# The first two chunks of a Strassen feed-forward: order of adds, tiles, splits and copies

## What is computed

```
def swiglu(h, w_gate, w_up, w_down):
    return (jax.nn.silu(h @ w_gate) * (h @ w_up)) @ w_down

def reference(x, ...):
    for i in range(DEPTH):                       # DEPTH = 2
        hn = rms_norm(x, norm_mix_g[i])
        x = x + gmlp_mixer(...)  or  x + chunk_attention(...)
        hn = rms_norm(x, norm_ffn_g[i])
        x = x + swiglu(hn, ffn_w_gate[i], ffn_w_up[i], ffn_w_down[i])
    return rms_norm(x, final_g)
```

## Time and profile before

| | us |
|---|---|
| median of 3 runs | 2608.01 (2607.97 to 2608.17) |
| the profiled execution, its own time | 2607.87 |
| its span in the trace | 2606.1 |
| TensorE busy | 2459.5 (94%) |
| VectorE / ScalarE / GpSimd busy | 1684.9 / 1002.8 / 1295.1 |
| mean granted TensorE clock | 0.986 |

### The profile page before, as it was taken

One profiled execution on the slowest core, in us unless ns is written; L12 is line 12 of the kernel. 1 busy time (PEld: TensorE's weight loads), 2 busy tenths in 40 slices (PEclk: granted clock), 3 DMA queues, 4 the chain that ended last, 5 costly groups with the idle time before them and its releaser, 6 DMA issues. The chain is left out here.

```text
span 2606.1 us, 36363 instructions
## 1 busy us (share of the span) xinstructions
PE 2459.5 (94%) x11464; PEld 2024.2 (78%) x11464; DVE 1684.9 (65%) x2669; ACT 1002.8 (38%) x1815; POOL 1295.1 (50%) x908
## 2 busy tenths in 40 slices
PE   8998999999899999998889999999888999999997
PEld 6887888877688888876767777777766888888876
DVE  5246666667576777666756666676675667677756
ACT  4112111224344333331465555566642334433323
POOL 4242223222788787877212012221125877888776
PEclk9998999999999999999999999999999999999998
DMA  4223122111111211111110011111011111111111
GB/s 161 92 98 98 61 76 74 58 35 37 44 58 48 62 51 57 56 55 42 59 35 25 26 42 42 42 38 39 13 41 29 57 56 56 48 60 53 57 57 65
DMA packets 70522, 143.74 MB, mean 55 GB/s; under 512 B 7312, under 2 KB 17696, under 8 KB 69936
## 3 DMA queue, kind: packets, MB, share of 16 engines
q1 hardware_dynamic: 52912, 119.72, 14.3%
q10 hardware_dynamic: 17536, 23.07, 2.6%
HBM read 130.13 MB, written 12.63 MB: 55 GB/s over the span
## 5 line engine op out<-in xcount | busy, mean ns | idle before, releaser
L703 POOL TENSOR_TENSOR a_lo<-raw_block,a_hi 128x512 fp32r<-128x512 f32 x364 | 510.3, 1402 | 152.1 <-ACT a_hi L1554 128.0
L665 POOL TENSOR_SCALAR w_hi<-raw 128x1024 fp32r<-128x1024 f32 x80 | 91.1, 1139 | 847.0 <-PE bank L914 601.0
L1554 ACT ACTIVATE a_hi<-raw_block 128x512 fp32r<-128x512 f32 x312 | 195.9, 629 | 342.5 <-PE bank L914 143.7
L912 PE MATMUL bank<-T_hi,a_hi 128*128 128x512 f32 x672 | 264.0, 393 | 7.8 <-issue 7.1
L914 PE MATMUL bank<-T_hi,a_lo 128*128 128x512 f32 x672 | 263.1, 391 | 0.0
L913 PE MATMUL bank<-T_lo,a_hi 128*128 128x512 f32 x672 | 262.7, 391 | 0.0
L912 PE MATMUL bank<-B_hi,a_hi 128*128 128x512 f32 x576 | 225.2, 391 | 2.6 <-DVE h_full L2004 1.8
L914 PE MATMUL bank<-B_hi,a_lo 128*128 128x512 f32 x576 | 224.2, 389 | 0.0
L913 PE MATMUL bank<-B_lo,a_hi 128*128 128x512 f32 x576 | 224.2, 389 | 0.0
L667 POOL TENSOR_TENSOR w_lo<-raw,w_hi 128x1024 fp32r<-128x1024 f32 x80 | 198.4, 2480 | 6.7
L2004 DVE TENSOR_TENSOR h_full<-bank,h_full 128x512 f32<-128x512 f32 x54 | 37.3, 691 | 212.2 <-PE bank L914 211.8
(11 more groups left out here) (276 smaller groups left out, 6658.5 us busy)
## 6 DMA issues: line engine op xcount, KB each, us to landing
raw_block<-f_blocks_in SPq DMA_DIRECT2D x176, 256.0 KB, 2.6
raw<-w_units_in SPq DMA_DIRECT2D x80, 512.0 KB, 3.5
raw_block<-f_down_in SPq DMA_DIRECT2D x72, 256.0 KB, 3.0
v_raw<-v_scratch ACTq DMA_DIRECT2D x16, 512.0 KB, 3.9
bias<-rel_scratch ACTq DMA_DIRECT2D x8, 640.0 KB, 3.5
x<-x_t_in SPq DMA_DIRECT2D x16, 256.0 KB, 5.7
v_scratch<-atmp ACTq DMA_DIRECT2D x16, 256.0 KB, 2.6
v_scratch<-full ACTq DMA_DIRECT2D x16, 256.0 KB, 2.5
```

The lines of the kernel that those rows point to most:

```text
L665: pool.tensor_scalar(w_hi[slot][:, :], raw[r][:, :], 1.0, 1.0, ALU.mult, ALU.mult).then_inc(w_split, 1)
L703: pool.tensor_tensor(out, full, r32(hi), ALU.subtract).then_inc(made, 1)
L912: pe.matmul(out, lh, rh, start=start, stop=False, skip_group_check=read_between)
L1554: act.activation(a_hi[pos][:, :], src[:, :], ACT.Copy).then_inc(w.left_hi, 1)
```

## The change

- **Chunk 0, half 0 of the down product:** VectorE does the residual adds earlier among its preparations for half 1: two by two before, now single adds between `scaled`, `difference` and `right_lo`. The same instructions, another order.
- **Chunk 0, half 1:** TensorE takes B22 of feature tile 1 (banks 1, 3) in the k loop and tile 0 (banks 0, 2) behind it, bank by bank. All that follows takes tile 1 first: the additions, silu, the product, the high and low parts, and the down product. VectorE makes the sums T2, T3, T4 for all four k ahead of it, where two of four stood behind it. T3's low parts 1 to 3 now stand behind the first `cadd` of chunk 1.
- **Chunk 1's gate group** becomes a middle group: GpSimd leaves seven high parts to ScalarE's `left_high`, which gets them at the end of chunk 0. GpSimd and the last load start from product 10 (banks 1 and 3 done), not 12; ScalarE's high parts in slots 4 to 6 still wait for 12. SyncE loads the blocks for the up group in the order of a middle group, and TensorE waits by its numbers.
- **Chunk 1, ScalarE:** the high parts A11, A12 of the up group go behind the copy of bank 0 after S2, and the one of S2 behind the copy of bank 1 after S3, where each stood ahead of it.
- The counts of the semaphores `made` and `left_hi` are renumbered for every later chunk; nothing else of those is touched.

```diff
-MID_MADE = 20 + GROUP
+MID_MADE = 20 + MID
...
+AT_G0_SECOND = AT_G1 - 1
...
-sp.wait_ge(s.prod, 12)
+sp.wait_ge(s.prod, 10)
 block(1, 3, 3)
...
-gate_up(1, 1, lambda op: MADE_SECOND + MADE[op], first_order)
+gate_up(1, 1, lambda op: middle(1, AT_G0_SECOND, MID, MID_MADE + MIDDLE[op]), order)
...
-        pool.wait_ge(s.left_hi, middle(it, at, 7, slot + 1))
+        pool.wait_ge(s.left_hi, middle(it, at, 7, 7 + slot + 1))
...
-        pool.wait_ge(s.prod, N_PROD.first)
+        pool.wait_ge(s.prod, 10)
...
-        group(3, lambda op: MADE_SECOND + MADE[op], lambda op: None)
+        middle_group(it, AT_G0_SECOND)
...
         for up in range(2):
+            tile(bank[2 * up + 1], 5 + 2 * up, "B22", k, False, k == 3, s.prod if k == 3 else None)
+    for up in range(2):
+        for k in range(4):
             tile(bank[2 * up], 4 + 2 * up, "B22", k, False, k == 3, s.prod if k == 3 else None)
-    for k in range(4):
-        for up in range(2):
-            tile(bank[2 * up + 1], 5 + 2 * up, "B22", k, False, k == 3, s.prod if k == 3 else None)
-    down(0, "first", 1, 8, ((0, 3), (1, 4)))
+    down(0, "first", 1, 8, ((1, 3), (0, 4)))
...
-    for k in range(2):
+    for k in range(4):
         right_hi("T2", k, full_lo["T2"], 20 + 3 * k + 1)
         right_hi("T4", k, full_lo["T4"], 20 + 3 * k + 3)
     act.wait_ge(w.cadd, 1)
+    silu(held[:, 1, :], hidden_part(h_full, 1, 1))
+    hi(0, 3, 1, 1)
+    act.wait_ge(w.prod, 10)
+    for pos in range(2):
+        left_high(1, AT_G0_SECOND, pos)
+    act.wait_ge(w.cadd, 3)
     silu(held[:, 0, :], hidden_part(h_full, 0, 1))
-    hi(0, 3, 0, 1)
-    act.wait_ge(w.cadd, 3)
-    silu(held[:, 1, :], hidden_part(h_full, 1, 1))
-    hi(0, 4, 1, 1)
-    for k in range(2, 4):
-        right_hi("T2", k, full_lo["T2"], 20 + 3 * k + 1)
-        right_hi("T4", k, full_lo["T4"], 20 + 3 * k + 3)
+    hi(0, 4, 0, 1)
+    for pos in range(2, 4):
+        left_high(1, AT_G0_SECOND, pos)
+    act.wait_ge(w.prod, 12)
+    for pos in range(4, 7):
+        left_high(1, AT_G0_SECOND, pos)
     for k in range(4):
         right_hi("T3", k, full_lo["T3"], 32)
...
-        if kind == "second":
-            product(0, {slot: op for op, slot in SLOT.items()}[pos])
-            left_high(it, AT_G1, pos)
-        else:
-            product(0, ORDER[pos])
-            left_high(it, AT_D, pos)
+        product(0, ORDER[pos])
+        left_high(it, AT_G1 if kind == "second" else AT_D, pos)
...
     snap(bank[0], gated[0])
-    behind_gate(0)
     if kind != "second":
+        behind_gate(0)
         right_high(it - 1, "T1")
         right_high(it - 1, "T3")
-    behind_gate(1)
+        behind_gate(1)
     product(0, "S2")
     snap(bank[0], gated[1])
+    if kind == "second":
+        behind_gate(0)
+        behind_gate(1)
     act.wait_ge(w.cadd, N_CADD.at(it, 1))
     silu(gated[0][:, :], gated[0])
     if kind != "second":
         right_high(it - 1, "T2")
         right_high(it - 1, "T4")
-    behind_gate(2)
+        behind_gate(2)
     product(0, "S3")
     snap(bank[1], gated[2])
+    if kind == "second":
+        behind_gate(2)
     behind_gate(3)
     behind_gate(4)
...
-    for k in range(5):
-        if k < 4:
-            scaled(k, k, full_lo["T3"][:, k, :])
-            scaled(k, 4 + k, b22_full[:, k, :])
-        if k:
-            right_lo("T1", k - 1, full_lo["T2"], 8 + 2 * k)
-        if k < 4:
-            difference(full_lo["T2"], full_lo["T3"], full_lo["T2"], k, 8 + 3 * k + 1)
-        if k:
-            right_lo("B22", k - 1, b22_full, 8 + 2 * k)
-        if k < 4:
-            add(0, "first", 0, 0, 2 * k)
-            add(0, "first", 0, 0, 2 * k + 1)
-    t2_t3_t4(0)
-    t2_t3_t4(1)
+    def t3(k):
+        scaled(k, k, full_lo["T3"][:, k, :])
+
+    def b22(k):
+        scaled(k, 4 + k, b22_full[:, k, :])
+
+    def t1(k):
+        difference(full_lo["T2"], full_lo["T3"], full_lo["T2"], k, 8 + 3 * k + 1)
+
+    def t1_lo(k):
+        right_lo("T1", k, full_lo["T2"], 8 + 2 * (k + 1))
+
+    def b22_lo(k):
+        right_lo("B22", k, b22_full, 8 + 2 * (k + 1))
+
+
+    t3(0)
+    b22(0)
+    t1(0)
+    add(0, "first", 0, 0, 0)
+    add(0, "first", 0, 0, 1)
+    t1_lo(0)
+    add(0, "first", 0, 0, 2)
+    b22_lo(0)
+    add(0, "first", 0, 0, 3)
+    t3(1)
+    b22(1)
+    add(0, "first", 0, 0, 4)
+    t1(1)
+    add(0, "first", 0, 0, 5)
+    t3(2)
+    t1_lo(1)
+    add(0, "first", 0, 0, 6)
+    b22_lo(1)
+    add(0, "first", 0, 0, 7)
+    b22(2)
+    t1(2)
+    t3(3)
+    t1_lo(2)
+    b22_lo(2)
+    b22(3)
+    t1(3)
+    t1_lo(3)
+    b22_lo(3)
+    for k in range(4):
+        t2_t3_t4(k)
     t2_t4_lo(0)
     dve.wait_ge(w.prod, 9)
-    cadd(held[:, 0, :], bank[0])
+    cadd(held[:, 1, :], bank[1])
     dve.wait_ge(w.prod, 10)
-    cadd(held[:, 2, :], bank[2])
+    cadd(held[:, 3, :], bank[3])
     t2_t4_lo(1)
     dve.wait_ge(w.cadd, 2)
     dve.wait_ge(w.act, 3)
-    times(held[:, 2, :], 0, 1)
+    times(held[:, 3, :], 1, 1)
+    t2_t4_lo(2)
     dve.wait_ge(w.prod, 11)
-    cadd(held[:, 1, :], bank[1])
-    lo(0, 3, 0, 1)
+    cadd(held[:, 0, :], bank[0])
+    lo(0, 3, 1, 1)
     dve.wait_ge(w.prod, 12)
-    cadd(held[:, 3, :], bank[3])
+    cadd(held[:, 2, :], bank[2])
     dve.wait_ge(w.cadd, 4)
     dve.wait_ge(w.act, 4)
-    times(held[:, 3, :], 1, 1)
-    t2_t3_t4(2)
-    lo(0, 4, 1, 1)
-    add(0, "first", 1, 8, 0)
-    add(0, "first", 1, 8, 1)
-    t2_t3_t4(3)
-    add(0, "first", 1, 8, 2)
-    add(0, "first", 1, 8, 3)
-    t2_t4_lo(2)
-    add(0, "first", 1, 8, 4)
-    add(0, "first", 1, 8, 5)
-    t2_t4_lo(3)
-    add(0, "first", 1, 8, 6)
-    add(0, "first", 1, 8, 7)
+    times(held[:, 2, :], 0, 1)
+    right_lo("T2", 3, full_lo["T2"], 16 + 2 * 3 + 2)
+    lo(0, 4, 0, 1)
     for k in range(4):
+        add(0, "first", 1, 8, k)
+    right_lo("T4", 3, full_lo["T4"], 16 + 2 * 3 + 2)
+    for k in range(4, KT):
+        add(0, "first", 1, 8, k)
+    right_lo("T3", 0, full_lo["T3"], 24 + 1)
+    dve.wait_ge(w.prod, N_PROD.at(1, PROD["A12"]))
+    dve.wait_ge(w.snap, N_SNAP.at(1, 1))
+    cadd(gated[0][:, :], bank[1])
+    for k in range(1, 4):
         right_lo("T3", k, full_lo["T3"], 24 + k + 1)
...
-    product(0, "A12")
-    snap(1)
-    cadd(gated[0][:, :], bank[1])
     if kind != "second":
+        product(0, "A12")
+        snap(1)
+        cadd(gated[0][:, :], bank[1])
```

More of the change, by code:

```diff
@@ L132 @@
 N_PROD, N_SNAP, N_CADD = Count(12, 14), Count(4, 6), Count(4, 6)
-MADE_SECOND, MADE_LAST = 20, middle(LATE, AT_D_LATE, MID, MID_MADE + MID)
+MADE_FIRST, MADE_LAST = 20, middle(LATE, AT_D_LATE, MID, MID_MADE + MID)
 def ge(eng, sem, value):
@@ L1151, in first_chunk @@
                     spread(norm, 1)
-                    pe.wait_ge(s.made, MADE_SECOND)
+                    pe.wait_ge(s.made, MADE_FIRST)
                     down(0, "first", 0, 0, ((0, 1), (1, 2)))
@@ L1175, in made @@
                         elif kind == "second" and g == 0:
-                            pe.wait_ge(s.made, MADE_SECOND + MADE[op])
+                            pe.wait_ge(s.made, middle(it, AT_G0_SECOND, MID, MID_MADE + MIDDLE[op]))
                         else:
@@ L1212, in one @@
                             swapped = kind == "late" and g == 1
-                            by_gpsimd = kind == "second" and g == 0
                             for op in ("S4", "A22") if swapped else ("A22", "S4"):
                                 made(g, "lo " + op)
-                                slot = SLOT[op] if by_gpsimd else ORDER.index(op)
+                                slot = ORDER.index(op)
                                 if op == "A22":
```

## The result

| | us |
|---|---|
| changed kernel, median of 4 runs | 2587.68 (2584.94 to 2588.96) |
| kernel before, beside it | 2608.09 (2607.97 to 2610.88) |
| ratio | 0.9913, 95% interval 0.9898 to 0.9927 |
| profiled execution of the changed kernel, its time | 2588.96 |
| its span | 2586.8 (before 2606.1) |

The account below looks back on a forecast made before the run. TensorE's waits and slow clock around the first chunk's down product and second gate lose 16.5 us per feed-forward. Gate 6.3 us earlier (3.0 from adds) plus 4.6 gives 10.8, twice 21.6: 2607.87 becomes 2586.5, range 2576 to 2594.

Parts of the forecast that it names:

- Adds: Chunk 0, half 0 of the down product: TensorE's waits for residual adds go, 3.0 us won for each feed-forward.
- Tile 1 first: Chunk 0, half 1: hidden low parts ready at 654.3 and 659.3; TensorE idles 2.8 us first, then waits again.
- Low clock: Second half of the down product: 0.5 us added for slow clock after the first pause, between 0 and 2.
- GpSimd's early start: GpSimd's first sum at 649.1, amid VectorE's chain; SBUF-only VectorE instructions there cost 0.60 alone, up to 1.67 us beside it.
- B: Rival: VectorE and GpSimd hardly meet in half 1; gate at 663.1, 15.8 us for each feed-forward, 2576.5 us; chance 0.18.
- C: Rival: VectorE and GpSimd meet each time in half 1; gate at 671.2, 7.7 us each, 2592.5 us; chance 0.15.
- Pause before A22: Chunk 1's gate: ScalarE's copies ahead of high parts close TensorE's pause, 4.6 us won for each feed-forward, gate takes 19.0.
- The cover that I gave for the up group: Chunk 1's up group: GpSimd's low parts come early enough, A11 with 8 us of cover, S2 with 6; no stall.
- Sum: Up group starts 10.8 us earlier in the first feed-forward; twice, 21.6 us, time 2586.5; chance 0.55.
- Slower, by a longer round of GpSimd: Rival: chunk loops, TensorE waits for GpSimd in each of 25 groups, twice; 2636 us at 1 us a group; chance 0.05.

Follow-up runs that it names:

- e1: Kernel before with only VectorE's residual adds of half 0 in the new order; 2603.95 us, ratio 0.9979.
- e7: Changed kernel with VectorE's residual adds of half 0 back in the old order; 2594.76 us, ratio 0.9945.
- e12: Changed kernel once more, nothing altered, run on one chip with three follow-up kernels; 2587.83 us, ratio 0.9918.
- e2: Kernel before with only ScalarE's new order in chunk 1 (bank copies ahead of high parts A11, A12, S2); 2602.30 us, ratio 0.9972.
- e4: Changed kernel with GpSimd and the load of the last raw block waiting for product 12 again, not 10; 2581.10 us, ratio 0.9892.
- e5: Changed kernel with the last load still from product 10, but GpSimd waiting for VectorE's second hidden low part; 2581.49 us, ratio 0.9893.
- e3: Changed kernel with ScalarE's old order in chunk 1 (high parts A11, A12, S2 ahead of the copies); 2588.21 us, ratio 0.9919.
- e9: e4 with ScalarE's copy of bank 3 ahead of S2's high part in chunk 1's up group; 2584.09 us (three executions), ratio 0.9900.
- e6: Changed kernel with three of VectorE's T low parts moved behind steps of the hidden tiles' chain; 2588.04 us, ratio 0.9920.

## Why the prediction was right, point by point

- **Adds.** Forecast 3.0 us for each feed-forward; 2.7 (e1) and 3.5 (e7 against e12) by the times, 3.0 by the way to T1 at either clock. TensorE waits for no add. The profiled execution of the changed kernel shows less, 1.2 us at T1's first matmul: its first matmuls of the down product step by 0.43 us (619.39), the 1.2 GHz level, after the same 1.74 us pause for the norm that has the 2.4 GHz level behind it in the kernel before. The order of the adds doesn't decide it: with the old order the lower level is there in e2 and e7 too.
- **Tile 1 first.** VectorE's time line was forecast for the low parts at 654.3 and 659.3; TensorE's restarts are at 654.46 and 659.52. But TensorE's data was 1.85 us late (653.35 for 651.5, the clock above), and the chain with it, so from there it was 1.8 us faster than I had it: the first pause was 0.94 us and not 2.8. That the restarts agree to 0.2 us is luck, two errors that cancel; the order of events is what was right. GpSimd's first sum came 1.9 us later too, at 650.97, and waited for VectorE, not VectorE for it. Of the four instructions behind, two took 1.7 us as in the earlier trace rows, two about 1.
- **Low clock.** I added 0.5 us, between 0 and 2. From the second restart to the gate 36 matmuls took 9.92 us where 8.2 would do: 1.7, at the 1.2 GHz level (0.63 us for the one at 662.16). The clock fell after the second pause, not the first. This is most of the 1.4 us by which the gate (669.44 for 668.0) and the up group (688.48 for 687.0) were late. It isn't the rule: behind pauses of the same length it did not fall in the second feed-forward (1971.65), nor in either one of e12.
- **GpSimd's early start.** That it costs was forecast, and so were its bounds B and C. That it costs more than it brings was not seen, though the numbers stood there: with the chain undisturbed, rival B has the gate at 663.1, and TensorE wants GpSimd's last low part 18 us after GpSimd was through. B's way from T1 to the gate, 33.3 us (629.8 to 663.1), is what e4 and e5 show (33.4). B's 10 us against the forecast were too much, 6.5 measured (e5 against e12), mostly because the chain beside GpSimd was not as bad as forecast (36.2 us in e12, 38.2 forecast) and by 0.7 us because the pause in the up group is longer.
- **Pause before A22.** It went, and 19.04 us for the gate is what was forecast. The reason was half right: the copies' order is enough for the gate (e2, first feed-forward), but not needed beside the middle group and the early start (e3). The cover that I gave for the up group counted only low parts; ScalarE's copy of bank 3, behind the high part of S2 of the next group, was missed, and TensorE paused there for 0.72 us (702.96). GpSimd's 6.92 us of idle time from the new order (678.99) are what made it late.
- **Sum.** 21.6 forecast, 18.9 in the profiled execution (2607.87 to 2588.96), 20.4 between the medians, 22.7 by the ratio. That it is so close is partly luck. Neither the lower clock on the way to T1 (1.3 to 1.6 us for each feed-forward) nor the loss in the up group (0.8) was in the sum, and the chain that was 1.8 us shorter than forecast paid for them.
- **Slower, by a longer round of GpSimd.** Nothing of it: the slices of the chunk loop are full. A late GpSimd does carry over a group or two (e2, e9), but no further.

## What to carry to other kernels

When a helper engine may start earlier, ask who else uses its port at that time: here GpSimd's first low part was ready 14 us before TensorE's gate (655.55 and 669.44), and the early start cost 6.5 us (4.3 by the stretch behind T1) in the chain that TensorE did wait for. A pause caused by an engine that is late isn't closed by reordering the queue in between, it moves to the next group; the order helps only to bridge until the engine has caught up. And the new order can itself make that engine late, when what it waits for is moved back. And a part is to be tested both alone and by leaving it out: the copies bring 7.3 us alone and nothing beside the rest, the adds 5.5 and 7.0, and tile 1 first 7.3 us or nothing that the times can tell, by where GpSimd starts.

## What the runs showed of the hardware

A pause of TensorE of one length is followed by either clock. After the 1.74 us at the norm the next matmuls step by 0.23 us in the kernel before (618.76, then 619.08 and 619.32) and by 0.43 us in the changed one; over the way to T1 the lower level costs 1.3 to 1.6 us. Behind the 2.0 us before the second hidden tile the clock fell in one of four feed-forwards of this kernel, and behind e6's single 2.10 us in both of its two. This is probably a part of why executions of one kernel lie up to 10.7 us apart (2583.03 to 2593.71 for e12, 2598.73 to 2607.87 for e1), where the first three of the kernel before lay within 0.2; that it is the cause was not tested. Differences of 2 us between these kernels are not told apart for that reason. And of the two engines that share the port, the one that loses can be GpSimd: 2.88 us for an addition of 1.3.
